# Expert weights in two mixtures: up matrices in 2 MB transfers into seven double buffers, down matrices in 1 MB transfers into seven single ones

## The chip, the cores and the metric

The kernel runs on one core of one Trainium2 chip. The metric is the device time of one execution in microseconds (us), lower is better; the median of three runs is given. MB stands for 1024 KB wherever buffers and transfers are counted; GB/s in the profile is decimal, so that one MB at 421 GB/s takes 2.49 us.

## What is computed

Two transformer blocks on 256 tokens of width 1024, all in float32. The part around the change is the mixture of experts that ends each block:

```
# block 1: 32 experts, hidden width 256, top-2 inside the best of 4 groups
hid = silu(einsum('td,edf->tef', t, w1)) * einsum('td,edf->tef', t, w3)
out = einsum('tef,efd->td', hid * gate, w2)
# block 2: 16 experts, hidden width 1024, top-2 inside the best of 4 groups
for e in range(16):
    h = silu(t @ w_gate[e]) * (t @ w_up[e])
    y = y + gate_dense[:, e:e + 1] * (h @ w_down[e])
```

Ahead of each mixture stands a token mixer: gated delta rule and spatial gating in block 1, stick-breaking and dilated attention in block 2. Ahead of block 1 and in the mixers, dense weights are loaded through the same buffers.

## The kernel before

**Work of a mixture.** Every expert is used, on the tokens routed to it. A **slice** is 256 hidden columns of one expert: 2 MB of up weights (both up matrices, in two halves of 1 MB by input rows) and 1 MB of down weights. Mixture 1 has 32 slices (96 MB), mixture 2 has 64 (192 MB). `mixture_steps` groups experts in units by how many tokens they hold: a **single** is one expert, a **pair** two, a **quad** four, and the experts of a unit work side by side on TensorE in 128, 64 or 32 columns. So a step costs TensorE about the same whatever its width, while it needs 3, 6 or 12 MB of weights. Mixture 1 has 11 steps, one for each unit: pair, pair, pair, quad, pair, quad, quad, pair, quad, quad, pair. Mixture 2 has 32 steps, four for each of its units: pair, pair, single, pair, quad, single, pair, pair. Steps are counted from 0. The first units hold "fixed" experts, known at build time; the others hold experts ranked by their load, and their numbers are read by SyncE with a `value_load` after VectorE has raised `order_ready`.

**Order on TensorE** (`mixture`, `up`, `down` in the tensor block): for step t it runs the first half of up(t+1), turns the hidden rows of t (L1143), at a new unit combines the outputs of the unit before and gathers the tokens of a later one, runs the second half of up(t+1), then down(t). The last combine is followed by a check of whether some expert has more than 64 tokens (`overflow`); here none has.

**Buffers** (`slot_table`). A ring of 11 slots of 1 MB, and nine other places of 1 MB that are free in a mixture: `x_ctx`, `heads`, `masks`, `head_w`, `tokens`, `squares`, `normed`, `routing`, `places` (the profile shows them as xc, o_heads, first_w, head_w, arena, hc, hc, arena, arena). That is 20 MB. `JOINS` says what such a place waits for when it is used first: `tokens` the residual of the mixer, `squares` and `normed` the norm ahead of the routing, `routing` and `places` the end of the routing itself. Every slot is freed when TensorE has run its last matmul on it: a counter `slots_used` counts slots in the order of use, and `FREE_AT` is the count that a load waits for.

**Loads** (`load_mixture`, `load_step`, L506). SyncE issues all weight loads in one fixed order, one by one, and waits in `slot_free` ahead of each that its slot is free; what stands behind a load that waits, waits too. The order is up(0), then for each t up(t+1) and down(t). Rows of a load are 8 KB long on each of 128 partitions. TensorE waits for the four (pair) or eight (quad) up slots of a step in two lots: first halves of all experts, then second halves. Dense weights of block 2 (16 loads) follow mixture 1 in the same queue, and the first loads of mixture 2 follow these.

```
for k in range(4):                                  # up(), each half of a step
    for j in range(wide):
        ins = mm(out[half, :], x[:, 4 * part + k, half], w[j][:, k, :], ...)
```

## Time and profile before

| | |
|---|---|
| median of three runs | 1599.21 us (1595.12 to 1599.33) |
| the profiled execution, its own time | 1599.86 us |
| its span in the trace | 1598.2 us |
| granted TensorE clock, mean | 0.98 |
| TensorE matmuls busy | 1480.7 us (93%) |
| VectorE, ScalarE, GpSimd busy | 511.2, 331.3, 152.2 us |
| bytes moved | 402.96 MB, of them 381.92 on SyncE's queue |

Busy time is the time in which an engine has an instruction under way. The views give microseconds from the start of the span. A row of the timeline has the start, how long the merged stretch lasts, the engine (PE is TensorE, DVE VectorE, ACT ScalarE, SPq SyncE's sequencer issuing transfers), the source line, operation, output and inputs, their shape, how many instructions it merges, and in brackets the idle time before it and what ended it. All matmuls written with the helper `mm` have line L679. A stretch of windows lists busy time and count of each engine, then the granted TensorE clock, the busy share of the 16 DMA engines and GB/s. The clock has two levels here, 1.0 (2.4 GHz) and 0.5 (1.2 GHz).

### The profile page before, as it was taken

What the parts mean: (1) busy time and instruction counts of PE and PEld (TensorE: products, weight loads), DVE (VectorE), ACT (ScalarE), POOL (GpSimd) and SP (SyncE); (2) the same over time, 40 slices, a digit from 0 to 9 for tenths busy, and PEclk for the clock granted to TensorE, in tenths of its full rate; (3) what the DMA queues carried; (4) which work ended last, traced back from release to release, by engine and by line L of the source; (5) the groups of instructions that cost most, each with busy time, mean ns of one, the idle gap of its engine ahead of it and who ended that gap; (6) DMA issues with size and microseconds to landing.
All of it is one profiled execution on the core that took longest, in us unless ns stands there. A gap on an engine that the chain in (4) does not pass through costs nothing.

```text
span 1598.2 us, 21336 instructions
## 1 busy us (share of the span) xinstructions
PE 1480.7 (93%) x8241; PEld 968.3 (61%) x8241; DVE 511.2 (32%) x1081; ACT 331.3 (21%) x725; POOL 152.2 (10%) x170
## 2 busy tenths in 40 slices
PE   6899999999999999989998789999999998579996
PEld 2577777777588888865554359967443543134433
DVE  2567777667631311153222110053401111001002
ACT  2343343443331100021110011152100000000001
POOL 1334433344200000000000000000000000000000
PEclk9999999999999999999999999999999999899999
DMA  9711111111754435429999996305699999999992
GB/s 381 315 54 39 52 39 39 39 52 39 294 223 156 158 132 185 160 93 372 421 420 422 421 415 239 132 1 190 269 421 421 421 421 422 421 421 421 422 420 122
DMA packets 58573, 402.96 MB, mean 252 GB/s; under 512 B 6801, under 2 KB 6929, under 8 KB 12288
## 3 DMA queue, kind: packets, MB, share of 16 engines
q1 hardware_dynamic: 52704, 381.92, 59.3%
q0 software_dynamic: 5792, 19.95, 4.1%
q8 instruction: 55, 0.90, 0.2%
q14 instruction: 22, 0.18, 0.0%
HBM read 400.75 MB, written 1.10 MB: 251 GB/s over the span
## 4 chain that ended last, share of the span: by engine, by line
PE 73%; SPq 9%; DMA 6%; DVE 5%; issue 2%; ACT 2%; POOL 1%; DVEq 0%; ACTq 0%; POOLq 0%
PE bank L679 72%; SPq L506 9%; DMA ring<-in_moe 4%; DMA first_w<-in_moe 2%; ACT arena L1435 1%; DVE arena L1874 1%; POOL arena L621 1%; PE bank L1143 1%; DMA xc<-in_xc 1%; DMA decay_rows<-arena 0%; ACT hc L1435 0%; DVE arena L1863 0%; DVE arena L1865 0%; DVE arena L1868 0%; DVE arena L1869 0%
## 5 line engine op out<-in xcount | busy, mean ns | idle before, releaser
L679 PE MATMUL bank<-arena 128*128 128x128 f32 (+6 forms) x3088 | 488.5, 326 | 34.9 <-DVE arena L1865 15.6
L679 PEld LDWEIGHTS bank<-arena 128*128 128x128 f32 (+3 forms) x3088 | 383.1, 184 | 163.1 <-issue 73.8
L1435 ACT ACTIVATE arena<-bank 128x256 f32<-128x256 f32 (+2 forms) x374 | 161.9, 448 | 1073.1 <-PE bank L679 797.9
L679 PE MATMUL bank<-ring,arena 128*64 128x512 f32 (+2 forms) x1288 | 330.6, 630 | 38.3 <-DMA ring<-in_moe 22.1
L679 PEld LDWEIGHTS bank<-ring,arena 128*64 128x64 f32 (+2 forms) x1288 | 99.1, 136 | 207.2 <-issue 206.5
L679 PE MATMUL bank<-hc,head_w 128*128 128x512 f32 (+1 forms) x384 | 161.6, 523 | 0.5 <-DVE hc L1798 0.5
L2218 DVE TENSOR_TENSOR arena<-arena,bank 128x256 f32<-128x256 f32 x43 | 18.1, 421 | 340.3 <-ACT arena L1435 340.3
L679 PE MATMUL bank<-arena,ring 128*128 128x256 f32 x416 | 93.2, 380 | 1.5 <-DVE arena L1993 1.2
L679 PE MATMUL bank<-hc,ring 128*128 128x256 f32 x416 | 91.2, 379 | 0.0
L679 PEld LDWEIGHTS bank<-arena,ring 128*128 128x128 f32 x416 | 78.7, 190 | 13.9 <-DVE arena L1993 1.6
L679 PEld LDWEIGHTS bank<-hc,ring 128*128 128x128 f32 x416 | 78.4, 190 | 11.1 <-issue 0.8
L679 PE MATMUL bank<-hc,arena 128*64 128x512 f32 (+2 forms) x216 | 79.5, 638 | 0.9 <-DVE arena L2214 0.9
L1435 ACT ACTIVATE arena<-arena 128x512 f32<-128x512 f32 (+4 forms) x140 | 66.5, 507 | 41.9 <-DVE arena L1815 25.3
L1895 DVE TENSOR_TENSOR arena<-bank,first_w 128x512 f32<-128x512 f32 x80 | 55.3, 692 | 55.4 <-PE bank L679 53.1
L679 PEld LDWEIGHTS bank<-hc,head_w 128*128 128x128 f32 x384 | 63.8, 192 | 14.5 <-issue 10.9
L679 PE MATMUL bank<-first_w,arena 128*64 128x512 f32 (+3 forms) x152 | 64.7, 558 | 6.6 <-DMA ring<-in_moe 5.2
L2214 DVE COPY arena<-bank 128x512 f32<-128x512 f32 x19 | 13.1, 692 | 169.5 <-PE bank L679 169.4
L679 PE MATMUL bank<-head_w,arena 128*64 128x512 f32 (+3 forms) x176 | 64.4, 505 | 1.1 <-DVE arena L2214 1.1
L1813 DVE SCALAR_TENSOR_TENSOR arena<-arena,vec 128x512 f32<-128x512 f32 (+1 forms) x72 | 65.0, 903 | 1.2
L626 POOL TENSOR_TENSOR arena<-arena,first_w 128x512 f32<-128x512 f32 x40 | 55.0, 1375 | 101.6 <-PE bank L679 60.4
L679 PE MATMUL bank<-o_heads,arena 128*64 128x512 f32 (+2 forms) x120 | 55.8, 609 | 3.2 <-DMA ring<-in_moe 2.3
L679 PE MATMUL bank<-xc,arena 128*64 128x512 f32 (+2 forms) x120 | 55.8, 609 | 0.0
(273 smaller groups left out, 1281.8 us busy)
## 6 DMA issues: line engine op xcount, KB each, us to landing
ring<-in_moe SPq DMA_DIRECT2D x161, 1024.0 KB, 23.4
ring<-in_dense SPq DMA_DIRECT2D x59, 1024.0 KB, 10.4
arena<-in_moe SPq DMA_DIRECT2D x40, 1024.0 KB, 24.2
hc<-in_moe SPq DMA_DIRECT2D x27, 1024.0 KB, 24.6
head_w<-in_moe SPq DMA_DIRECT2D x15, 1024.0 KB, 19.8
xc<-in_moe SPq DMA_DIRECT2D x15, 1024.0 KB, 26.8
o_heads<-in_moe SPq DMA_DIRECT2D x15, 1024.0 KB, 23.7
first_w<-in_moe SPq DMA_DIRECT2D x15, 1024.0 KB, 20.9
```

What stands on the lines that cost most here:

```text
L506: sp.dma_start(into, rows_[part % len(rows_)][:, at:at + GROUP]).then_inc(sem_, 16)
L621: nc.gpsimd.tensor_tensor(beta_half[1], beta_half[1], et[1], ALU.mult).then_inc(s["back_half"], 1)
L626: nc.gpsimd.tensor_tensor(levels[k % 2], coupling, times(M(f"off{k}"), TT), ALU.mult).then_inc(s["level_masked"], 1)
L679: return nc.tensor.matmul(out, lhsT, rhs_, start=start, stop=stop, **kw)
L1143: ins = nc.tensor.transpose(bank[4 + step_no % 2][:, f * P:(f + 1) * P], hid[step_no % 2][:, f * P:(f + 1) * P], M("ident"))
L1435: return nc.scalar.activation(out, in_, func, **kw)
L1813: link(stt(c3, src, wgt, c3, ALU.mult, ALU.add))
L1874: stt(flat(conv[0]), flat(conv[0]), float(P) ** -0.5, flat(norms[0]), ALU.mult, ALU.mult).then_inc(s["normed"], 1)
L1895: tt_(group_of(picked, g), grown(g), times(M(f"pick{k + 1}"), 4), ALU.mult).then_inc(s["picked"], 1)
L2214: cp(x_cols[u % 2][:, 4:8, :].rearrange("p a b -> p (a b)"), bank[7][:, :]).then_inc(s["x_copied"], 1)
L2218: tt_(hid[step_no % 2], act_h[step_no % 2], bank[4 + step_no % 2][:, FS:2 * FS], ALU.mult).then_inc(s["hid_ready"], 1)
```

## The change

- Up weights of one slice are loaded in one transfer of 2 MB (rows of 16 KB on each partition) by `load_up`, into one of seven **double** homes: five neighbouring pairs of ring slots (0-1, 2-3, 4-5, 6-7, 8-9), and `tokens` and `squares`, each now 2 MB (`squares` takes all of `hc`, so `normed` is gone). Down weights are loaded as before, 1 MB each, by `load_down`, into seven **single** homes: ring slot 10, `head_w`, `x_ctx`, `heads`, `masks`, `routing`, `places`. 7 x 2 + 7 = 21 MB.
- A double home is free when the second half of its slice has been used. In `up_view` both halves wait for the whole 2 MB, so the first half of a quad waits for 8 MB, and no longer for 4.
- `mixture_loads` sets the order of the loads: as before, but with down(2) of the first expert ahead of up(3), and in mixture 2 also up(3) of the first expert, down(2) of the second and down(3) of the first.
- `y_rows`, `act_h`, `hid` and `hid_T` have one buffer each where they had two; ScalarE and VectorE wait for the one buffer (`hid_ready`, `h_turned`, `combined`).
- VectorE waits for the last `combined` of a mixture behind the overflow check, and no longer ahead of it.

```diff
-UP_SLOTS = {"quad": 8, "pair": 4, "single": 2}
-DOWN_SLOTS = {"quad": 4, "pair": 2, "single": 1}
+DOUBLE = {home: (home, home + 1) for home in range(0, RING - 1, 2)}
+DOUBLE.update({"tokens": ("tokens",), "squares": ("squares",)})
...
+def mixture_loads(m):
+
+    steps = STEPS[m]
+    count = [WIDTH[step[0]] for step in steps]
+    turns = [("up", 0, j) for j in range(count[0])]
+    for t in range(len(steps)):
+        if t + 1 < len(steps):
+            turns += [("up", t + 1, j) for j in range(count[t + 1])]
+        turns += [("down", t, j) for j in range(count[t])]
+    sooner = [("down", 2, 0)] if m == 0 else [("down", 2, 0), ("up", 3, 0), ("down", 2, 1), ("down", 3, 0)]
+    at = turns.index(("up", 3, 0))
+    return turns[:at] + sooner + [turn for turn in turns[at:] if turn not in sooner]
...
+        for what, t, j in mixture_loads(m):
+            if what == "up":
+                take(double, ("up", m, t, j), ("up", m, t, j, 1))
+            else:
+                take(single, ("down", m, t, j), ("down", m, t, j, 0))
...
+            def load_up(m, step_no, j, row):
+
+                sem_ = slot_free(("up", m, step_no, j))
+                sp.dma_start(double_at(HOME["up", m, step_no, j]), row[:, 0:2 * GROUP]).then_inc(sem_, 16)
...
+                def up_view(step_no, j, part):
+                    what = ("up", m, step_no, j)
+                    pe.wait_ge(landed[HOME[what]], LANDED_AT[what])
+                    return double_at(HOME[what])[:, part * GROUP:(part + 1) * GROUP].rearrange("p (k f) -> p k f", k=4)
...
-                        w = [slot_view("up", step_no, wide * part + j).rearrange("p (k f) -> p k f", k=4) for j in range(wide)]
+                        w = [up_view(step_no, j, part) for j in range(wide)]
...
                 def silu(step_no):
-                    act.wait_ge(slots_used, SLOT["up", m, step_no, UP_SLOTS[steps[step_no][0]] - 1] + 1)
-                    act_fn(act_h[step_no % 2], bank[4 + step_no % 2][:, 0:FS], ACT.Silu).then_inc(s["silu_made"], 1)
+                    act.wait_ge(slots_used, USED["up", m, step_no, WIDTH[steps[step_no][0]] - 1, 1])
+                    if step_no >= 1:
+                        act.wait_ge(s["hid_ready"], tb + step_no)
+                    act_fn(act_h, bank[4 + step_no % 2][:, 0:FS], ACT.Silu).then_inc(s["silu_made"], 1)
...
-                    if u >= 2:
-                        act.wait_ge(s["combined"], ub + u - 1)
-                    act_fn(y_rows[u % 2][:, 0:512], bank[6][:, :], ACT.Copy).then_inc(s["out_rows_copied"], 1)
+                    if u >= 1:
+                        act.wait_ge(s["combined"], ub + u)
+                    act_fn(y_rows[:, 0:512], bank[6][:, :], ACT.Copy).then_inc(s["out_rows_copied"], 1)
...
-                dve.wait_ge(s["combined"], ub + UNITS[m])
                 n_links = link.n
                 with dve.If(overflow(dve, m)):
+                    dve.wait_ge(s["combined"], ub + UNITS[m])
                     every_token(m)
                 assert link.n == n_links
+                dve.wait_ge(s["combined"], ub + UNITS[m])
```

The order of instructions on SyncE's queue at the two places where a stream of loads starts again. **First place:** the start of mixture 1, from the last load ahead of the routing. Before (the shape is partitions x floats, so 2048 is 1 MB; `arena` is `tokens` in the first row and `routing`, `places` further on, `hc` is `squares` and `normed`; TENSOR_LOAD reads an expert's number):

```order
L506 DMA arena<-in_moe 128x2048
L517 TENSOR_LOAD arena
L517 ISA x2
L517 TENSOR_LOAD arena
L517 ISA x2
L517 TENSOR_LOAD arena
L517 ISA x2
L517 TENSOR_LOAD arena
L517 ISA x2
L506 ISA
L506 DMA hc<-in_moe 128x2048
L506 ISA
```

With the change, behind the four reads (4096 is 2 MB; `hc` is `squares`, the ring pairs are 4-5, 6-7, 8-9, `arena` is `routing`):

```order
L555 DMA hc<-in_moe 128x4096
L555 ISA
L555 DMA ring<-in_moe 128x4096
L555 ISA
L555 DMA ring<-in_moe 128x4096
L555 ISA
L555 DMA ring<-in_moe 128x4096
L560 DMA arena<-in_moe 128x2048
```

Where eight loads of 1 MB carried the up weights of the first quad, four loads of 2 MB carry them now, and the 1 MB load into `routing` stands behind the fourth of them. That fourth one goes into ring pair 8-9, which held up(1) of the first expert; the next two (into pairs 0-1 and 2-3) are up(4).

**Second place:** the start of mixture 2. Before:

```order
L506 DMA hc<-in_moe 128x2048
L506 DMA head_w<-in_moe 128x2048
L506 DMA ring<-in_moe 128x2048 x7
L506 DMA xc<-in_moe 128x2048
L506 DMA o_heads<-in_moe 128x2048
L506 DMA first_w<-in_moe 128x2048
L506 DMA ring<-in_moe 128x2048 x4
L506 DMA arena<-in_moe 128x2048
L506 DMA hc<-in_moe 128x2048 x2
L506 DMA head_w<-in_moe 128x2048
L506 DMA ring<-in_moe 128x2048 x2
```

With the change:

```order
L555 DMA ring<-in_moe 128x4096 x4
L560 DMA first_w<-in_moe 128x2048
L560 DMA head_w<-in_moe 128x2048
L555 DMA ring<-in_moe 128x4096
L555 DMA arena<-in_moe 128x4096
L560 DMA ring<-in_moe 128x2048
L560 DMA xc<-in_moe 128x2048
L560 DMA o_heads<-in_moe 128x2048
L555 DMA hc<-in_moe 128x4096
L560 DMA arena<-in_moe 128x2048 x2
L555 DMA ring<-in_moe 128x4096
```

The second `hc` row of before is `normed` used for the second time, behind the first use of up(0); what stands ahead of it comes to 18 MB. With the change 19 MB stand ahead of the two `arena` rows (`routing`, `places`), and the ring pair behind them is the first that waits for up(0) to be used.

## Rows read from the trace of the kernel before

**Rows 1.** Page, part 2: GB/s in 40 slices of 40 us
```profile
GB/s 381 315 54 39 52 39 39 39 52 39 294 223 156 158 132 185 160 93 372 421 420 422 421 415 239 132 1 190 269 421 421 421 421 422 421 421 421 422 420 122
```
**Rows 2.** Windows: both mixtures' streams; columns as under the table above
```profile
745.00:945.00 200.00, 178.64 (x1146) 95.98 (x1143) 39.39 (x90) 21.95 (x45) 0.00 (x0) 0.96 1.01 421
1145.00:1545.00 400.00, 367.64 (x1744) 154.82 (x1742) 37.74 (x88) 29.66 (x70) 0.00 (x0) 0.97 1.01 421
```
**Rows 3.** Timeline of SyncE's issues, from mixture 1's first load to its restart
```profile
598.54 0.33 SPq L506 DMA_DIRECT2D head_w<-in_moe  x1
...
692.33 0.42 SPq L506 DMA_DIRECT2D arena<-in_moe  x1
722.34 0.94 SPq L506 DMA_DIRECT2D hc<-in_moe  x2
```
**Rows 4.** Windows of 1 us at the restart of mixture 2's stream
```profile
1132.00:1133.00 1.00, 1.00 (x8) 0.35 (x6) 0.89 (x5) 0.00 (x0) 0.00 (x0) 1.00 0.92 123
1133.00:1134.00 1.00, 1.00 (x6) 0.29 (x4) 0.90 (x6) 0.00 (x0) 0.00 (x0) 1.00 0.46 180
1134.00:1135.00 1.00, 1.00 (x6) 0.14 (x2) 0.71 (x3) 0.00 (x0) 0.00 (x0) 1.00 0.98 418
```
**Rows 5.** Timeline of TensorE: second halves of steps 1 and 2, mixture 1
```profile
736.50 3.65 PE L679 MATMUL bank<-ring,arena 128*64 128x512 f32 x16
...
754.34 4.08 PE L679 MATMUL bank<-ring,arena 128*64 128x512 f32 x17
```
**Rows 6.** Timeline of TensorE: first half of mixture 1's last step
```profile
905.16 3.65 PE L679 MATMUL bank<-ring,arena 128*64 128x512 f32 x16 [1.35 <-DMA ring<-in_moe]
```
**Rows 7.** Timeline of SyncE's issues in mixture 2
```profile
955.70 0.33 SPq L506 DMA_DIRECT2D hc<-in_moe  x1
...
1105.84 26.16 SPq L506 DMA_DIRECT2D hc<-in_moe  x2
...
1137.34 1.02 SPq L506 DMA_DIRECT2D arena<-in_moe  x2
...
1288.08 14.73 SPq L506 DMA_DIRECT2D ring<-in_moe  x5
```
**Rows 8.** Timeline of VectorE: the instruction that raises order_ready in mixture 2
```profile
1134.60 0.17 DVE L2055 CAST arena<-arena 128x14 uint32<-128x14 f32 x1
```
**Rows 9.** Timeline of TensorE in mixture 2: slot rows, then steps 13 and 14
```profile
1135.02 1.98 PE L679 MATMUL bank<-arena,ones 128*128 128x512 f32 x4
...
1295.23 4.08 PE L679 MATMUL bank<-ring,arena 128*64 128x512 f32 x17
...
1306.05 7.09 PE L679 MATMUL bank<-ring,arena 128*64 128x512 f32 x32
```
**Rows 10.** Timeline of TensorE: the last step of mixture 2
```profile
1559.69 3.65 PE L679 MATMUL bank<-ring,arena 128*64 128x512 f32 x16 [0.94 <-DMA ring<-in_moe]
...
1568.24 0.44 PE L1143 MATMUL bank<-first_w,arena 128*128 128x128 f32 x2
1569.57 0.61 PE L679 MATMUL bank<-o_heads,arena 128*64 128x512 f32 x1 [0.89 <-DMA first_w<-in_moe]
```
**Rows 11.** Timeline of TensorE and VectorE: last combine of each mixture, and what follows
```profile
936.52 3.72 PE L679 MATMUL bank<-arena 128*128 128x256 f32 x16 [0.82 <-DVE arena L2226]
...
941.76 3.23 DVE L2299 SCALAR_TENSOR_TENSOR xc<-bank,mod,xc 128x256 f32<-128x256 f32 x8 [5.29 <-issue]
...
1574.01 3.72 PE L679 MATMUL bank<-arena 128*128 128x256 f32 x16 [0.79 <-DVE arena L2226]
...
1578.64 2.74 DVE L2391 SCALAR_TENSOR_TENSOR xc<-xc,bank 128x256 f32<-128x256 f32 x8 [4.68 <-PE bank L679]
```
**Rows 12.** Windows: the load of xc, in rows of 16 KB, at the start
```profile
5.00:6.00 1.00, 0.00 (x0) 0.00 (x0) 0.00 (x0) 0.00 (x0) 0.00 (x0) 1.00 1.01 426
5.00:8.00 3.00, 0.00 (x0) 0.00 (x0) 0.00 (x0) 0.00 (x0) 0.00 (x0) 1.00 1.01 423
```
**Rows 13.** Window: TensorE at half clock in the down part of step 9
```profile
920.00:927.00 7.00, 5.61 (x32) 1.49 (x32) 0.00 (x0) 0.00 (x0) 0.00 (x0) 0.54 1.01 421
```

More of the change, by code:

```diff
@@ new lines, in slots_in_order_of_use, with parts, take, join @@
+def slots_in_order_of_use(m):
+    steps = STEPS[m]
+    def parts(what, t):
+        n = WIDTH[steps[t][0]]
+        return [(what, m, t, j, part) for part in range(2 if what == "up" else 1) for j in range(n)]
+    uses = parts("up", 0)
+    for t in range(len(steps)):
+        if t + 1 < len(steps):
+            uses += parts("up", t + 1)
+        uses += parts("down", t)
+    return uses
+def slot_table():
+    dense = [("dense", g, 0) for g in range(FIRST_GROUPS + SECOND_GROUPS)]
+    uses = dense[:FIRST_GROUPS] + slots_in_order_of_use(0) + dense[FIRST_GROUPS:] + slots_in_order_of_use(1)
+    used = {what: n + 1 for n, what in enumerate(uses)}
+    home_of, landed_at, free_at, joins = {}, {}, {}, {}
+    filled = {home: base for home, (_, base) in SHARED_SEMS.items()}
+    single = [(home, 0) for home in range(RING)]
+    double = []
+    def take(free, what, last_use):
+        home, freed = free.pop(0)
+        filled[home] = filled.get(home, 0) + 16
+        home_of[what], landed_at[what], free_at[what] = home, filled[home], freed
+        free.append((home, used[last_use]))
+    def join(home, what, sem, value):
+        assert home_of[what] == home, (home, what, home_of[what])
+        joins[what] = (sem, value)
+    def paired(free):
+        at = dict(free)
+        pairs = [(home, max(at.pop(h) for h in of)) for home, of in DOUBLE.items() if all(h in at for h in of)]
+        return sorted(pairs, key=lambda f: f[1]), sorted(at.items(), key=lambda f: f[1])
+    for g in range(FIRST_GROUPS):
+        for at, home in ((RING, "x_ctx"), (G0 // BLOCKS, "heads"), (G0 // BLOCKS + 1, "masks")):
+            if g == at:
+                single.insert(0, (home, 0))
+        take(single, ("dense", g), ("dense", g, 0))
+    join("x_ctx", ("dense", RING), "modulated", 1)
+    join("heads", ("dense", G0 // BLOCKS), "gdn_normed", 4)
+    join("masks", ("dense", G0 // BLOCKS + 1), "gdn_normed", 4)
+    for m in range(2):
+        double, single = paired(single)
+        double += [("tokens", 0), ("squares", 0)]
+        single += [("routing", 0), ("places", 0)]
+        if m == 0:
+            single.insert(0, ("head_w", 0))
+        for what, t, j in mixture_loads(m):
[3 more added lines that the diff above has]
+                take(single, ("down", m, t, j), ("down", m, t, j, 0))
+        first_use = {}
+        for what, t, j in mixture_loads(m):
+            first_use.setdefault(home_of[what, m, t, j], (what, m, t, j))
+        join("tokens", first_use["tokens"], *(("rest_taken", 5 * KT), ("out2_made", KT))[m])
+        join("squares", first_use["squares"], *(("rows_copied", 4), ("ln_var", 1))[m])
+        join("routing", first_use["routing"], *(("slots_spread", 1), ("order_ready", 2))[m])
+        join("places", first_use["places"], *(("slot_rows_made", 2), ("slot_rows_made", 4))[m])
+        if m == 0:
+            join("head_w", first_use["head_w"], "sgu_taken", KT)
+            single += [(h, freed) for home, freed in double for h in DOUBLE[home]]
+            single = sorted([f for f in single if f[0] not in ("tokens", "squares", "routing", "places")], key=lambda f: f[1])
+            for g in range(FIRST_GROUPS, FIRST_GROUPS + SECOND_GROUPS):
+                take(single, ("dense", g), ("dense", g, 0))
+    return used, landed_at, home_of, free_at, joins
@@ L164 @@
+USED, LANDED_AT, HOME, FREE_AT, JOINS = slot_table()
 SECOND_G = FIRST_GROUPS
@@ L518, in rows_of @@
                     return [row_of(m, w, ranked, i) for w in who]
[L520 to L527 removed]
+                for what, t_, j in mixture_loads(m):
+                    row = rows_of(t_)[j]
+                    if what == "up":
+                        load_up(m, t_, j, row)
+                    else:
+                        load_down(m, t_, j, row)
             def load_all_tokens(m):
@@ L1158, in down @@
                         wide = WIDTH[kind]
-                        w = [slot_view("down", step_no, j).rearrange("p (f d) -> p f d", f=2) for j in range(wide)]
+                        w = [down_view(step_no, j) for j in range(wide)]
                         for f in range(2):
```

164 lines of the change are left out of this document (59 added, 105 removed).

## The prediction

> **What bounds the kernel now.** I read the page's GB/s line first: 421 GB/s without a gap through most of both mixtures, far less elsewhere [rows 1]. Then windows over the two stretches: the DMA engines' share is 1.01, and 421 GB/s is the mean of 200 and of 400 us, while TensorE is idle for 21 and 32 us in them [rows 2]. So each mixture ends when its weights have arrived, and its end can be written as a sum: the moment at which the stream of loads runs again after the routing, plus the MB that are left, at 2.49 us each. Three things can move it: when the stream starts again and with how much in place, whether it ever runs dry, and its rate. TensorE's own work lies inside, except behind the last loads.
>
> A load is not moving as soon as it is issued. Mixture 2's stream starts again with the second of the two `hc` loads, issued at about 1131.6; the three microseconds to 1135 carry 123, 180 and 418 GB/s [rows 4, 7], as much as full rate from 1133.2 on. I count 1.6 us from issue to full rate.
>
> **Mixture 1, the stream.** Before, 16 loads of 1 MB are issued from 598.5 to 692.3, and the next at 722.3 [rows 3], so the stream runs from 723.9 with 80 MB left: 80 x 2.49 = 199.2, to 923.1. Nothing runs dry [rows 2].
>
> With the change 17 MB are in place by then (up 0, 1, 2, down 0, 1 and one of down 2), which is 1 MB or **2.5 us less** to do. But the queue then holds `squares` and ring pairs 4-5 and 6-7, whose slices have been used, and behind them pair 8-9, which is free only when TensorE has run the second half of step 1: the sixteen matmuls at 736.5 to 740.1 [rows 5]. Six MB last from 723.9 to 738.9; the seventh starts at 740.1 + 1.6 = 741.7. **Dry for 2.8 us.** Then 5 MB are free (pair 8-9, `routing`, pair 0-1) and last until 754.2. Next is pair 2-3, which waits for the second half of step 2: sixteen of the seventeen matmuls from 754.3 on, to 757.9 [rows 5]; start at 759.5. **Dry for 5.3 us.** Before, each half was freed by itself, and eight loads could be out where the new order waits on one. Check: at 759.5 the order has 28 MB behind it and 68 left, 169.3 us, end at 928.8, which is **5.7 us later** than 923.1 (2.8 + 5.3 - 2.5 = 5.6).
>
> **Mixture 1, TensorE behind it.** Up(10) is followed in the queue by 4 MB of down(9), 10.0 us. Before, its halves landed apart; now TensorE starts it when all is there and runs first half, turn, combine, second half: 3.6 + 0.4 + 3.7 + 3.6 = 11.3 us [rows 6, 11]. Down(9) starts **1.2 us later** than its data.
>
> **Mixture 2, the stream.** Before: 18 loads from 955.7 to 1105.8 [rows 7], running from 1133.2 with 174 MB left, 433.3 us, end at 1566.5. With the change 19 MB are in place; `routing` is next and waits for `order_ready`, raised at 1134.8 [rows 8], so the stream runs from 1136.4, and `places` joins at 1137.0, when the slot rows are made [rows 9]. The second load of the ring pairs behind them is free too, so this start costs 3.2 - 2.5 = 0.7 us. The buffers are full again at the single unit, where TensorE takes only 3 MB a step. Up(16) of the second expert has 84 MB ahead of it, which arrive by 1136.4 + 65 x 2.49 = 1298.3. Its pair, 6-7, is freed by the second half of step 13, from 1295.2 to 1298.8 [rows 9]; start at 1300.4. Before, too, SyncE stands still in this place (five issues in 14.7 us) [rows 7], but with enough loads out to bridge it. Dry for 2.1 us. Four MB later, 1310.4, pair 0-1 waits for the second half of step 14: 1306.05 is two halves, the first of them frees it at 1309.6 [rows 9]; start at 1311.2, dry for 0.8 us. Left are 104 MB, 259.0 us: end at 1570.2, **3.7 us later**.
>
> **Mixture 2, TensorE behind it.** The last loads are up(31), two of down(30), two of down(31). Before, the second half of up(31) began at 1559.7 and down(31) at 1569.6, 9.9 us for 4 MB, each part on its data [rows 10]. Now both halves wait for 1559.7, and from there come two halves, a turn, down(30), a turn and the copy of the turned rows (1568.2 to at least 1569.1): 3 x 3.6 + 0.4 + 0.9 = 12.1 us. **2.2 us.**
>
> **VectorE's wait.** The last combines end at 940.2 and 1577.7; VectorE goes on at 941.8 and 1578.6 [rows 11], because it reads the count of tokens only then. With the change that read is done before. I take **-2.0 us**; at most 2.4, at least 0.8, as ScalarE and TensorE still do such a read of their own.
>
> **The rate.** Rows of 16 KB occur once, in the load of `xc` at the start: 423 GB/s over 3 us, 426 over the best of them, against 421 with rows of 8 KB [rows 12, 2]. So the gain on up weights lies between nothing and 1.2%; I take 1%, between the two windows. It counts only behind the last dry stretch, since what comes sooner ahead of one only lengthens it: two thirds of 68 + 104 MB, 114 MB or 284 us, **-2.8 us** (ends: 0 and -3.4).
>
> The Trainium skill, "DMA: Bandwidth & Descriptors", section Bandwidth, has a fixed 2 us for each transfer and 341 GB/s at 1 MB against 425 at 16 MB. By that, half as many up transfers would be worth many microseconds more than I take. This trace disagrees for queued loads: 1 MB loads back to back already run at 421 GB/s [rows 2].
>
> **Costs nothing:** the single `act_h`, `hid`, `hid_T` and `y_rows`. ScalarE's silu of t+1 needs the second half of up(t+1), which TensorE runs after the turn of t, so `hid_ready` and `h_turned` have come; copying outputs of a unit comes after a whole down, and the combine of the unit before stands ahead of it. If TensorE's order were another, each would cost the copy, 0.4 to 0.7 us a step. SyncE's issues halve for up weights; it only waits [rows 7].
>
> **Sum:** 5.7 + 1.2 + 3.7 + 2.2 - 2.0 - 2.8 = **+8.0 us**, on the profiled execution's own 1599.9, so 1607.9. That execution is 0.7 above the median of the runs, so I say **1607 us**.
>
> **Rivals.**
> 1. *Part of the delay is repaid* (0.21). TensorE waits in few long pieces in place of many short ones. In the down part of step 9 the granted clock was 0.54 over 7 us, right behind such a wait, which cost 7 x 0.46 = 3.2 us [rows 13]; with down(9) now behind 11 us of work instead of behind an idle time this can vanish, and a rate gain at its upper end adds 0.6: +4.2, about 1603.5, within 0.3%. Against it: new waits of over 10 us in the quads (8 MB is 20 us) are worse for the clock.
> 2. *Faster* (0.11): rows of 16 KB run clearly faster once the queue is full. Without the rate the sum is +10.8, and each percent gives 2.8 us, so the change breaks even at 3.9%, 437 GB/s, and is faster by over 0.3% from 5.6%, 445 GB/s; with 6% it would be 1593. For it: only 3 us of such rows were seen, beside other loads. Against: those read 423 and 426 [rows 12]. The Trainium skill, same page, section Bandwidth, gives 435 GB/s as the ceiling of the sixteen ports; by it this case ends below break-even.
> 3. *The rows are cut up and the rate stays* (0.07): +10.8, 1610.
> 4. *Colder* (0.11): each mixture's last steps hold one more such piece at half clock, 3.2 us each: +14.4, about 1613.5.
>
> **Chances.** The forecast has 0.50, and with rivals 3 and 4 slower has 0.68; no change 0.21, faster 0.11. A measurement of this kernel can tell about 0.3%, 4.8 us, from no change. The forecast's own range is 1604 to 1611 (rate 0 to 1.2%, VectorE's ends, each dry stretch a microsecond either way); taking in rivals 1, 3 and 4 the range is 1599 to 1614.
>
> **What would show it.** Right: GB/s falls short of 421 around 739 and 755, and around 1299 and 1311; the stream of mixture 2 starts again 3 us later than before; the last combine of mixture 1 begins some 6 us later, that of mixture 2 some 4 us later within its mixture; VectorE goes on at once behind them. In the quads of mixture 2 TensorE waits once a step for over 10 us in place of twice for 6. Wrong: no dip at those places (pairs free sooner than I count), a rate over 430 GB/s in the steady part, or mixture 1 ending no later than before.

## The result, and the profile after

| | before | with the change |
|---|---|---|
| median of the runs | 1597.9 us (5 runs, 1595.1 to 1599.3) | 1605.0 us (5 runs, 1601.8 to 1608.4) |
| ratio | | 1.0046, 95% interval 1.0033 to 1.0059 |
| the profiled execution, own time and span | 1599.86, 1598.2 us | 1601.81, 1600.1 us |

The change costs 7.3 us by the ratio (0.46%), 7.1 by the medians. A second set of six runs of the same kernel, later in the study, gave 1.0045 (1.0031 to 1.0060). The profiled execution of the changed kernel is the fastest of its five, so the two profiles differ by only 1.9 us where the medians differ by 7. I compare by stages, therefore, and not by spans.

The page's GB/s in 40 slices, changed kernel (it answers to [rows 1]):

```profile
GB/s 386 311 51 39 52 39 43 36 52 39 305 232 148 145 131 158 54 251 320 426 424 427 415 412 203 132 5 245 301 426 426 421 379 426 424 426 426 425 424 87
```

Two things are to be seen: the level of most full slices is 424 to 427 where it was 420 to 422, and two slices fall out of it, 320 (slice 19, 720 to 760; 372 before) and 379 (slice 33, 1280 to 1320). Windows show why: the places at which the forecast had the queue run dry or start late, and between them the two streams of [rows 2]. Columns are as there, the last two the DMA share and GB/s:

```profile
736.00:738.00 2.00, 2.00 (x12) 0.69 (x10) 0.00 (x0) 0.31 (x1) 0.00 (x0) 1.00 0.19 74
738.00:740.00 2.00, 2.00 (x12) 0.60 (x10) 1.79 (x6) 0.07 (x1) 0.00 (x0) 1.00 0.64 147
750.00:752.00 2.00, 2.00 (x19) 1.88 (x20) 0.08 (x1) 0.60 (x1) 0.00 (x0) 1.00 0.67 287
752.00:754.00 2.00, 2.00 (x10) 0.58 (x10) 0.61 (x1) 0.00 (x0) 0.00 (x0) 1.00 0.00 0
754.00:756.00 2.00, 2.00 (x12) 0.72 (x10) 0.05 (x1) 0.38 (x1) 0.00 (x0) 1.00 0.00 0
756.00:758.00 2.00, 2.00 (x12) 0.70 (x10) 1.89 (x6) 0.00 (x0) 0.00 (x0) 1.00 0.87 213
745.00:945.00 200.00, 176.98 (x1140) 95.92 (x1139) 39.37 (x90) 22.25 (x46) 0.00 (x0) 0.95 0.98 411
1132.00:1134.00 2.00, 2.00 (x8) 0.68 (x4) 0.97 (x4) 0.38 (x1) 0.00 (x0) 1.00 0.47 94
1134.00:1136.00 2.00, 2.00 (x10) 0.63 (x10) 1.76 (x4) 0.00 (x0) 0.00 (x0) 1.00 0.94 389
1145.00:1545.00 400.00, 360.98 (x1728) 152.69 (x1726) 37.48 (x87) 29.61 (x70) 0.00 (x0) 0.95 1.00 420
1294.00:1296.00 2.00, 2.00 (x12) 0.72 (x10) 0.00 (x0) 0.00 (x0) 0.00 (x0) 1.00 0.35 147
1296.00:1298.00 2.00, 2.00 (x12) 0.69 (x10) 1.10 (x4) 0.38 (x1) 0.00 (x0) 1.00 0.50 106
1298.00:1300.00 2.00, 2.00 (x12) 0.61 (x10) 1.81 (x5) 0.00 (x0) 0.00 (x0) 1.00 0.76 303
1308.00:1310.00 2.00, 2.00 (x13) 0.58 (x9) 0.07 (x1) 0.00 (x0) 0.00 (x0) 1.00 0.84 246
```

Counted as time at 426 GB/s that is missing: 2.9 us around 738, 5.7 around 754, 3.4 around 1297, 0.8 around 1309. The stream of mixture 2 is at full rate from 1133.7 (1136 less 483 x 2 / 426), and the mixture itself (VectorE's first gather instruction) began 2.5 us sooner in this execution, so against it the restart is some 3 us later than before. SyncE's issues in mixture 1 show the load on which the queue stands (answering to [rows 3]):

```profile
721.19 16.92 SPq L555 DMA_DIRECT2D ring<-in_moe  x3
738.22 0.37 SPq L560 DMA_DIRECT2D arena<-in_moe  x1
739.93 16.03 SPq L555 DMA_DIRECT2D ring<-in_moe  x2
756.22 0.33 SPq L560 DMA_DIRECT2D arena<-in_moe  x1
```

The third and the fifth of these ring loads are the ones that wait for a second half of a step, and downs behind them (L560) are issued at once when they are out: those had been free for longer.

Behind the streams, TensorE at the last up of mixture 2, and VectorE's last copy of mixture 1 and first operation after it (answering to [rows 10, 11]):

```profile
1558.46 1.09 PE L731 MATMUL bank<-hc,arena 128*64 128x512 f32 x1 [2.92 <-DMA ring<-in_moe]
```

```profile
936.07 0.69 DVE L2287 COPY arena<-bank 128x512 f32<-128x512 f32 x1 [7.43 <-PE bank L731]
940.58 1.66 DVE L2361 SCALAR_TENSOR_TENSOR xc<-bank,mod,xc 128x256 f32<-128x256 f32 x4 [3.81 <-PE bank L731]
```

TensorE waits for the whole 2 MB of a slice; VectorE goes on 4.51 us after the start of its last copy, released by TensorE. TensorE's waits for DMA after 700 us, in total, times, longest:

```profile
PE bank L731 <- DMA ring<-in_moe: 54.4, 8, 15.9
PE bank L731 <- DMA arena<-in_moe: 5.8, 1, 5.8
PE bank L731 <- DMA head_w<-in_moe: 2.6, 1, 2.6
```

Before, the ring's were 32.3 us in 10 waits, the longest 6.3:

```profile
PE bank L679 <- DMA ring<-in_moe: 32.3, 10, 6.3
```

### The profile page after: what moved, and what is told of

Same layout as the page of the kernel before. It is cut to its first block, busy times and chain, and to the rows that moved or that the text cites. A ratio compares the mean times of both kernels' runs of the same rounds, so it can differ in the third digit from the quotient of the medians.

```text
span 1600.1 us, 21159 instructions
## 1 busy us (share of the span) xinstructions
PE 1478.0 (92%) x8241; PEld 963.7 (60%) x8241; DVE 511.1 (32%) x1081; ACT 331.0 (21%) x725; POOL 152.2 (10%) x170
## 4 chain that ended last, share of the span: by engine, by line
PE 79%; DMA 10%; DVE 5%; issue 2%; ACT 2%; POOL 1%; SPq 1%; DVEq 0%; ACTq 0%; POOLq 0%
PE bank L731 78%; DMA ring<-in_moe 8%; ACT arena L1492 1%; PE bank L1200 1%; DVE arena L1933 1%; DMA head_w<-in_moe 1%; POOL arena L673 1%; DMA arena<-in_moe 1%; DMA xc<-in_xc 1%; ACT hc L1492 0%; DVE arena L1922 0%; DVE arena L1924 0%; DMA decay_rows<-arena 0%; DVE arena L1927 0%; DVE arena L1928 0%
## 5 line engine op out<-in xcount | busy, mean ns | idle before, releaser
L731 PE MATMUL bank<-arena 128*128 128x128 f32 (+7 forms) x3184 | 548.9, 335 | 47.6 <-DMA ring<-in_moe 20.8
L731 PEld LDWEIGHTS bank<-arena 128*128 128x128 f32 (+3 forms) x3184 | 399.3, 183 | 202.9 <-issue 116.6
L731 PE MATMUL bank<-ring,arena 128*64 128x512 f32 (+2 forms) x1232 | 336.7, 627 | 38.3 <-DMA ring<-in_moe 30.6
L731 PE MATMUL bank<-hc,arena 128*64 128x512 f32 (+1 forms) x208 | 101.0, 631 | 2.9 <-DMA ring<-in_moe 2.9
L731 PE MATMUL bank<-arena,ring 128*128 128x256 f32 x352 | 78.4, 380 | 1.5 <-DVE arena L2052 1.2
L731 PEld LDWEIGHTS bank<-hc,head_w 128*128 128x128 f32 x384 | 64.6, 194 | 16.8 <-issue 13.2
L731 PEld LDWEIGHTS bank<-arena,ring 128*128 128x128 f32 x352 | 66.6, 190 | 11.9 <-DVE arena L2052 1.6
L731 PE MATMUL bank<-head_w,arena 128*64 128x512 f32 (+2 forms) x168 | 60.6, 499 | 0.0
L731 PE MATMUL bank<-first_w,arena 128*64 128x512 f32 (+2 forms) x144 | 58.9, 539 | 1.6 <-DVE arena L1928 1.5
L731 PE MATMUL bank<-o_heads,arena 128*64 128x512 f32 (+2 forms) x112 | 50.5, 593 | 0.6 <-DMA first_w<-in_moe 0.6
L731 PE MATMUL bank<-xc,arena 128*64 128x512 f32 (+2 forms) x112 | 50.5, 593 | 0.0
## 6 DMA issues: line engine op xcount, KB each, us to landing
ring<-in_dense SPq DMA_DIRECT2D x60, 1024.0 KB, 10.5
```

Of the source, the lines that this page charges most:

```text
L731: return nc.tensor.matmul(out, lhsT, rhs_, start=start, stop=stop, **kw)
```

## The experiments

All were timed in five rounds, between runs of the kernel before (on these chips 1597.6 to 1597.8). Because the streams set the end, I also give the length of the mixtures themselves in each profile: from VectorE's first gather instruction to its last copy of outputs.

| kernel | median us | ratio to before, 95% | us | mixture 1, us | mixture 2, us |
|---|---|---|---|---|---|
| before | 1597.9 | | | 225.1 | 450.8 |
| the change | 1605.0 | 1.0046 (1.0033, 1.0059) | +7.3 | 228.0 | 455.7 |
| the change again | 1604.9 | 1.0045 (1.0031, 1.0060) | +7.2 | 228.2 | 455.9 |
| 1 wait put back | 1608.2 | 1.0057 (1.0043, 1.0071) | +9.1 | 230.6 | 455.9 |
| 2 two loads | 1608.7 | 1.0060 (1.0046, 1.0074) | +9.6 | 229.2 | 458.8 |
| 3 two waits | 1605.2 | 1.0041 (1.0027, 1.0054) | +6.6 | 227.3 | 457.1 |
| 4 list reordered | 1599.8 | 1.0013 (1.0004, 1.0022) | +2.1 | 226.2 | 452.4 |
| 5 two releases | 1598.1 | 1.0004 (0.9995, 1.0013) | +0.6 | 224.9 | 456.2 |
| 6 before, wait moved | 1595.9 | 0.9989 (0.9980, 0.9998) | -1.8 | 225.1 | 450.7 |
| 7 before, single buffers | 1597.6 | 1.0001 (0.9992, 1.0010) | +0.2 | 222.6 | 450.9 |
| 8 21 homes of 1 MB | 1589.0 | 0.9946 (0.9932, 0.9959) | -8.6 | 219.2 | 448.5 |
| 9 as 8, 16 MB ahead | 1594.4 | 0.9977 (0.9968, 0.9986) | -3.7 | 222.5 | 448.2 |
| 10 as 8, by slices | 1586.1 | 0.9930 (0.9917, 0.9943) | -11.2 | 217.5 | 448.3 |
| 12 as 5, reordered | 1595.9 | 0.9984 (0.9975, 0.9993) | -2.6 | 223.1 | 453.2 |

The column "us" is (ratio - 1) x 1597.7. Each has an interval of 1.4 to 2.2 us either way, and a difference of two has 2 to 3. One profile's mixture 1 can lie 2.5 us off another's of the same loads (kernels before and 7), see the last section.

**The change again** (experiment 11), unaltered.

> The changed kernel itself, on the chip of the last runs, as the foot of the ladder. Expected 1605, between 1603.5 and 1606.5.

**1. VectorE's wait put back.** The change, with

```
+                dve.wait_ge(s["combined"], ub + UNITS[m])
                 n_links = link.n
                 with dve.If(overflow(dve, m)):
-                    dve.wait_ge(s["combined"], ub + UNITS[m])
                     every_token(m)
-                dve.wait_ge(s["combined"], ub + UNITS[m])
```

> The changed kernel (1605.0) with VectorE's wait for the last combine put back ahead of the overflow check. Theory (the moved wait gave back about 2 us at the two mixture ends, the loads cost the rest): 1607, between 1606 and 1608, and in the trace the first VectorE operation after each mixture about 5.3 us after its combine's copy instead of 3.8. Rival (the check's value load was hidden anyway): 1605, no change.

It measured +1.8 against the change by the ratios (+3.2 by the medians, just above the expected range), where 2 was expected. The difference of two ratios is uncertain by 2 us or more, so this run alone doesn't show it. The profile has VectorE's operation after mixture 1 behind an idle time that nothing in the trace releases, 5.98 us after its last copy began:

```profile
940.27 0.69 DVE L2287 COPY arena<-bank 128x512 f32<-128x512 f32 x1 [7.43 <-PE bank L731]
946.25 3.23 DVE L2360 SCALAR_TENSOR_TENSOR xc<-bank,mod,xc 128x256 f32<-128x256 f32 x8 [5.29 <-issue]
```

**6. The kernel before, with only that wait moved** (the reverse edit).

> The kernel before with VectorE's wait moved into and behind the overflow check, nothing else. Theory: 1595.8, between 1595 and 1597, the first VectorE operation after each mixture's last combine 4.5 us after VectorE's last copy in both mixtures instead of 6.0 and 5.3. Rival (what lies between the mixtures absorbs it): 1597.8.

It measured -1.8 (interval -0.3 to -3.2), and in its profile the distance after mixture 1 is 4.51 us in place of the 6.0 of before, that after mixture 2 4.50 in place of 5.4:

```profile
935.23 0.69 DVE L2226 COPY arena<-bank 128x512 f32<-128x512 f32 x1 [7.43 <-PE bank L679]
939.74 3.23 DVE L2300 SCALAR_TENSOR_TENSOR xc<-bank,mod,xc 128x256 f32<-128x256 f32 x8 [3.81 <-PE bank L679]
```

Both sides and the distances in the traces agree: the moved wait is a gain of about 2 us, which the rest of the change hides.

**7. The kernel before, with single buffers.** `act_h`, `hid`, `hid_T`, `y_rows` as in the change, with its waits, for instance

```
-                    if u >= 2:
-                        act.wait_ge(s["combined"], ub + u - 1)
-                    act_fn(y_rows[u % 2][:, 0:512], bank[6][:, :], ACT.Copy)...
+                    if u >= 1:
+                        act.wait_ge(s["combined"], ub + u)
+                    act_fn(y_rows[:, 0:512], bank[6][:, :], ACT.Copy)...
```

> The kernel before with one act_h, one hid, one hid_T and one y_rows and the changed kernel's waits for them; loads as before. Theory (no step waits for them): 1597.8, between 1597 and 1599. Rival (the added waits of ScalarE and VectorE hold each step up by 0.1 us or more over 43 steps): 1602 or more.

+0.2, within 1.6 of nothing. The buffers that the change gives up had no use in this order of the work.

**2. Two loads for each double home.**

```
-                sp.dma_start(double_at(HOME["up", m, step_no, j]), row[:, 0:2 * GROUP]).then_inc(sem_, 16)
+                into = double_at(HOME["up", m, step_no, j])
+                for half in (slice(0, GROUP), slice(GROUP, 2 * GROUP)):
+                    sp.dma_start(into[:, half], row[:, half]).then_inc(sem_, 16)
```

(and 32 counts for an up's landing in the table)

> The changed kernel with each 2 MB up slice loaded as two transfers of 1 MB (rows of 8 KB) into the same double home, same order, freed and waited for as one. Theory (the rows of 16 KB are a gain of 1.2 percent on the queued stretches, hidden behind the loss): the steady rate falls from 426 to 421 GB/s, mixture 1 ends 2 us and mixture 2 3 us later, 1610, between 1608 and 1612. Rival (the rate does not matter or comes from the larger transfer being issued early, not from its rows): 426 GB/s stays, 1605. Rival (large transfers are the harm): 1600 or less.

1608.7, +2.3 us against the change by the ratios, +3.7 by the medians; the mixtures are 1.2 and 3.1 us longer than in the change's profile. Rows and issues are all that differ, and the page's level is back at 421:

```profile
GB/s 385 306 54 39 52 39 42 36 52 39 312 226 156 134 129 157 72 239 334 422 421 421 418 409 184 131 25 242 287 420 421 422 391 421 422 421 421 421 421 83
```

So the large transfers are a gain of about 1.2% in rate, and they are not what costs the time. Whether it is the longer rows or the fewer transfers that give it, this run can't tell: it changes both.

**3. Two loads, two waits.** Each half has its own count of landings, and `up_view` waits for its own part alone:

```
-                    pe.wait_ge(landed[HOME[what]], LANDED_AT[what])
+                    if part == 0:
+                        pe.wait_ge(landed[HOME[what]], LANDED_AT[what])
+                    else:
+                        pe.wait_ge(landed[LANDED_AT[(*what, 1)][0]], LANDED_AT[(*what, 1)][1])
```

> As the run before, with a semaphore for each 1 MB half, so that TensorE's first half of a step waits for the first halves alone; homes still freed as one. The loads stay in the slice order, so of a step of four TensorE still needs three and a half slices before it starts. Theory (landing granularity is the small part, 1 to 3 us at the ends of the mixtures): 1608, between 1606 and 1610, the last up of mixture 2 no longer waiting 2.9 us. Rival (landing of 2 MB at once is the main loss): 1602 or less.

It measured 1605.2, 0.8 below the range expected, and 3.0 us (ratios) or 3.5 (medians) below experiment 2, shared by both mixtures (1.9 and 1.7). The rival's 1602 was not reached. That the last up of mixture 2 would no longer wait did not come: TensorE waits 4.05 us there (4.79 in experiment 2).

**5. Two loads, two waits, two releases.** The first half of a home is free when the first half of its slice is used:

```
                 sp.dma_start(into[:, 0:GROUP], row[:, 0:GROUP]).then_inc(sem_, 16)
+                if FREE_AT[(*what, 1)] > 0:
+                    sp.wait_ge(slots_used, FREE_AT[(*what, 1)])
...
+            free_at[(*what, 1)] = freed
+            freed = first_freed[0] if first_freed else freed
+            free.append((home, used[last_use], used[(*last_use[:4], 0)]))
```

> The kernel with two transfers and two waits (1605.2), and now each half of a double home is also released by its own use: the first half by the first half of the step, one TensorE piece of 3.4 us to over 10 us sooner. Same order of the slices. Theory (the late release of first halves is the largest part of the loss): 1600.5, between 1599 and 1602.5; the dry stretch at 751 to 757 falls from 6 us to 3, those at 1294 to 1300 and 1308 to nothing. Rival (the order of the list, slices before halves, is the loss and the release is not): 1605.

1598.1, 5.9 us below experiment 3 by the ratios and 7.1 by the medians, sooner than the whole range that was expected. But the expected picture came only in part. Around 738 only 0.7 us is missing now (270 GB/s in 740 to 742), and 1.0 us near 1305 in place of the stretches at 1297 and 1309. The stretch at 752 to 760, which was to halve, is 5.4 us at 421 GB/s, as in experiment 3:

```profile
752.00:754.00 2.00, 2.00 (x18) 1.76 (x18) 0.21 (x1) 0.60 (x1) 0.00 (x0) 1.00 0.84 352
754.00:756.00 2.00, 2.00 (x12) 0.69 (x10) 0.48 (x1) 0.00 (x0) 0.00 (x0) 1.00 0.03 12
756.00:758.00 2.00, 2.00 (x12) 0.60 (x10) 0.18 (x1) 0.38 (x1) 0.00 (x0) 1.00 0.00 0
758.00:760.00 2.00, 2.00 (x12) 0.72 (x10) 1.86 (x7) 0.00 (x0) 0.00 (x0) 1.00 0.72 180
```

The list still goes slice by slice. The load of a first half goes out at 746.52, that of the second half behind it only at 757.50, and everything else stands behind it until then. The queue is one MB further when it stops, and that MB is the gain in mixture 1 (2.3 us in its stream, see the table of parts below). The gain of 6 to 7 us isn't to be found in the profile as a whole: the profiled execution is the slowest of the eleven (1600.9), and against experiment 3's its mixtures are 2.4 and 0.9 us shorter and the time between them 2.0.

**4. The change, with its list of loads reordered.** Homes, transfers and waits as in the change; downs with a free home go out ahead of an up that waits. In mixture 1 from step 1 on (u4.1 is the up slice of step 4's second expert):

```
+FIRST_LOADS = ("u0.0 u0.1 u1.0 u1.1 d0.0 d0.1 u2.0 d1.0 d1.1 u2.1 d2.0 u3.0 u3.1 d2.1 d3.0 u3.2 u3.3 u4.0 d3.1 d3.2 "
+               "u4.1 d3.3 u5.0 d4.0 u5.1 d4.1 d5.0 u5.2 u5.3 u6.0 d5.1 u6.1 d5.2 u6.2 d5.3 d6.0 u6.3 d6.1 u7.0 u7.1 "
...
+    for down, ahead_of in ((("down", 14, 0), ("up", 15, 1)), (("down", 15, 0), ("up", 16, 1)), (("down", 15, 1), ("up", 16, 3))):
+        turns.remove(down)
+        turns.insert(turns.index(ahead_of), down)
```

> The changed kernel with the same homes, 2 MB transfers and waits, and only the order of the load list changed, so that downs with a free home go out ahead of an up whose double home isn't released: in mixture 1 through most of the list, in mixture 2 three downs (steps 14, 15, 15). Theory (what costs is that the list blocks on a double home while single ones are free, so that the transfers run dry): the dry 6 us at 751 to 757 shrink to 2, those at 1294 to 1300 and 1308 to 1 together, 1597.5, between 1595 and 1600. Rival (fewer bytes can be in place whatever the order, since a double home is released 10 us later): dry stretches move but keep their sum, 1604 to 1606. Rival (single buffers make the steps slow): 1605.

1599.8: 5.2 us below the change, at the later end of what was expected. The transfers no longer stop around 754, but they do around 776, behind another up that waits:

```profile
752.00:754.00 2.00, 2.00 (x20) 2.00 (x20) 0.00 (x0) 0.31 (x1) 0.00 (x0) 1.00 0.96 410
754.00:756.00 2.00, 2.00 (x17) 1.59 (x18) 0.52 (x1) 0.28 (x1) 0.00 (x0) 1.00 0.97 410
776.00:778.00 2.00, 2.00 (x18) 0.56 (x12) 0.45 (x2) 0.38 (x1) 0.00 (x0) 1.00 0.00 0
```

At 426 GB/s some 6 us are missing in mixture 1's stream (3.5 of them at 772 to 780) where the change misses 9, and 2 where it misses 5 in mixture 2's. So the rival is half right here: the dry stretches move, but their sum shrinks. Mixture 1 is only 1.8 us shorter than the change's, mixture 2 3.3.

A home that is released sooner (experiment 5), or other loads sent ahead while it isn't (this one): by the medians either takes away most of the loss, and neither ends it.

**12. Both cures**: experiment 5 with the list of experiment 4.

> The two-frees kernel (1598.1) with the reordered list of the run that changed the order alone. Theory (two separate faults: the list, and homes split into ones for ups and ones for downs): the 3 us dry stretch at 753 to 757 vanishes, mixture 2 stays as it was, since there a down waits for the routing buffer from 1129 to 1134 with later homes free: 1595, between 1593.5 and 1596.5, and what is left against the kernel of 1 MB homes (1586.1) is the split. Rival (once halves are released by themselves the list no longer matters): 1598.

1595.9, 3.2 (ratios) or 2.2 us (medians) below experiment 5, as expected. Nothing is missing around 754, and 2.6 us at 776 to 784:

```profile
776.00:778.00 2.00, 2.00 (x16) 0.63 (x10) 0.85 (x3) 0.38 (x1) 0.00 (x0) 1.00 0.74 221
```

It stands where the kernel before stands with its wait moved (experiment 6, 1595.9).

**8. 21 homes of 1 MB.** The memory of the change, with `tokens` as two homes of 1 MB and `hc` as `squares` and `normed` again. Each home is loaded, waited for and released by itself. In mixture 1 two loads go ahead:

```
+    def parts(what, t):
+        n = WIDTH[steps[t][0]]
+        return [(what, t, j, part) for part in range(2 if what == "up" else 1) for j in range(n)]
...
+    moves = [[(('down', 2, 0, 0), ('up', 3, 0, 0)), (('down', 2, 1, 0), ('up', 3, 0, 0))], []][m]
...
+                 "tokens": area(5120, GROUP), "tokens2": area(5120 + GROUP, GROUP), "squares": flat(HS), "normed": flat(H),
```

> The changed kernel's memory (single buffers, tokens region of 2 MB, moved wait) but all homes of 1 MB, each filled by its own transfer, waited for and released by itself, halves in the order in which TensorE uses them (all first halves of a step, then all second ones), and in mixture 1 the two downs of step 2 ahead of step 3's first up, so that 18 MB stand in place before the routing is known. Theory (capacity helps, coarseness was the loss): against the kernel before -5 in mixture 1 (18 MB in place against 16), -2 in mixture 2 (one home more), -2 for the wait: 1589, between 1587 and 1592, at 421 GB/s. Rival (the added capacity lies where it isn't wanted): 1596, the wait's gain alone.

1589.0, as expected. The queue never runs dry and the rate is 421 from the first restart to the end:

```profile
GB/s 385 315 54 40 53 40 40 40 46 46 275 220 182 145 147 179 154 159 332 420 421 421 421 412 251 130 1 217 280 420 421 421 421 421 422 420 422 420 422 114
```

**9. As 8, without the two loads that go ahead.**

> The kernel of 21 homes of 1 MB (1589.0) without the two downs of step 2 ahead of step 3's first up in mixture 1: 16 MB in place before the routing is known instead of 18. Theory (mixture 1 is bound by the bytes left then, 2 MB at 421 GB/s are 5 us): 1594, between 1592.5 and 1595. Rival (the routing comes late enough that the two are made good by the ring): 1589.

1594.4, 5 us more, as 2 MB at 2.49 us say; mixture 1's stream is 5.0 us longer in the profile. What stands in place before the routing is known is worth its full transfer time. It is also a comparison with experiment 6: 1594.4 against 1595.9. That is 1.5 us by the medians and 1.9 by the ratios, no more than such a difference is uncertain by; mixture 2, where the 21st home was to give 2.5, is 2.5 shorter in the profile. The eleven executions here fall in two groups, five at 1591.5 to 1592.3 and six at 1594.4 to 1596.2.

**10. As 8, halves slice by slice** (`for j in range(n) for part in range(...)`).

> The kernel of 21 homes of 1 MB (1589.0) with the up halves loaded slice by slice as in the changed kernel, instead of all first halves and then all second ones. Theory (while the transfers never run dry the order within a step only moves TensorE's waits about): 1589 to 1590, the DMA's rows at 421 GB/s throughout; TensorE's longest wait 14 us instead of 6. Rival (the order of the halves is itself worth what the two-frees kernel lacked): 1591 to 1593.

1586.1: faster than expected by 2.9 us, and the best kernel of the study, 11.2 us below the kernel before. The theory was right that TensorE's waits change and wrong that the time doesn't. TensorE waits less often and longer:

```profile
PE bank L711 <- DMA ring<-in_moe: 20.1, 5, 6.4
PE bank L711 <- DMA hc<-in_moe: 13.8, 1, 13.8
PE bank L711 <- DMA head_w<-in_moe: 12.8, 1, 12.8
```

and at the end of mixture 1, where it works behind the last loads, the granted clock (third from the end) is 1.00, where experiment 8 has 0.89. Experiment 10, then experiment 8:

```profile
915.00:930.00 15.00, 13.42 (x76) 7.22 (x77) 2.64 (x5) 2.75 (x4) 0.00 (x0) 1.00 1.02 421
```

```profile
915.00:930.00 15.00, 12.75 (x67) 5.61 (x67) 1.38 (x2) 1.47 (x3) 0.00 (x0) 0.89 1.02 421
```

15 x 0.11 = 1.65 us, and mixture 1 is 1.7 shorter. I take the one for the other; with one profile of each it is not shown that the order of halves brings it (see the last section). The other 1.2 us lie between the mixtures (179.4 for 180.7 us), where the change itself shows either value in its two profiles. I can't say that the order causes that part.

## Why the prediction was right

The forecast was 1607, that is +8.0 us on a kernel before of 1599.2, with a loss as the likeliest case; it is 1605.0, +7.1 on 1597.9. The chain of experiments goes from the kernel before to the change in four steps, and each step can be set beside terms of the sum. (The steps add up to the change by construction; it is the single rows that bear on the forecast. The first step also holds the single buffers and the 21st MB.)

| terms of the prediction | forecast | measured by | by ratios (by medians) |
|---|---|---|---|
| both streams later | 5.7 + 3.7 = +9.4 | 3 against 6 | +8.3 (+9.3) |
| TensorE behind whole slices | 1.2 + 2.2 = +3.4 | 2 against 3 | +3.0 (+3.5) |
| VectorE's wait | -2.0 | 6 against before | -1.8 (-1.8) |
| rate | -2.8 | the change against 2 | -2.3 (-3.7) |
| sum | +8.0 | | +7.2 |

The profiles allow a finer account. Each mixture is three parts: from VectorE's first gather instruction to the full rate of the queue; the stream of loads from there until its last MB has moved, counted in windows of 2 us; and what TensorE does behind it, up to VectorE's last copy. Each part is good to some 0.3 us.

| profile | mixture 1: to full rate, stream, behind it | mixture 2 |
|---|---|---|
| before | 13.2, 199.2, 12.7 | 10.8, 433.9, 6.1 |
| 7 before, single buffers | 13.2, 199.1, 10.3 | 10.8, 433.9, 6.2 |
| the change | 13.6, 203.9, 10.5 | 13.8, 431.8, 10.1 |
| the change again | 13.6, 203.6, 11.0 | 14.0, 431.8, 10.1 |
| 3 two waits | 13.3, 204.8, 9.1 | 14.0, 434.2, 8.9 |
| 5 two releases | 13.2, 202.5, 9.1 | 14.2, 432.3, 9.8 |
| 12 as 5, reordered | 14.8, 199.1, 9.3 | 13.9, 431.5, 7.7 |
| 10 as 8, by slices | 13.3, 194.2, 10.0 | 10.8, 431.5, 6.1 |

The streams with their restarts were forecast, the rate taken off, 4.6 and 2.0 us later; they are 5.1 and 0.9 later (4.8 and 1.1 in the second profile of the change). That is the mechanism of the forecast, and it is right. What TensorE does behind them was forecast 1.2 and 2.2 longer and is 2.2 shorter and 4.0 longer. Here two effects of the clock enter that the sum does not have: the piece at half clock that the kernel before has at mixture 1's end and the change has not (3.2 us, rival 1), and one that the change has at mixture 2's end (1.7 us, part of rival 4). With both counted in, the forecast would be -2.0 and +3.9. So the good match of the total rests in part on luck: a gain and a loss that were priced as rivals are both in these profiles, and half cancel. By mixture the forecast was worse than its sum, +5.8 and +4.2 for +2.9 and +4.9, and its sign that mixture 1's last combine would come some 6 us later failed.

- **Mixture 1's stream.** The two dry stretches were put at 2.8 and 5.3 us and are 2.9 and 5.7. That pairs released by second halves are the cause was argued then. Experiment 5, which releases by halves, takes the first stretch away but for 0.7 us, and leaves the second, where a second half is still waited for in list order. Experiment 12, which also sends other loads ahead, takes the second away too (2.6 us are then missing at 776). So both bear on it, the late release and the list that waits on it.
- **Mixture 2's stream.** The restart was forecast 3.2 us later and came some 3 later; the dry stretches at 1298 and 1310, forecast at 2.1 and 0.8, are 3.4 and 0.8. The first is a microsecond more than worked out, about my margin; in the second profile of the change the two are 2.9 and 1.3.
- **TensorE behind it.** Measured in the mixtures' lengths, experiment 3 against 2: 1.9 and 1.7 us for the forecast's 1.2 and 2.2. Together right. Both have a granted clock of 0.86 in the last 25 us of mixture 2, so the difference is not the clock's. (4 MB are 10.0 us, so the forecast's own rows give 1.3 for its 1.2.)
- **VectorE.** Right, from both sides.
- **Rate.** I took 1% and the steady level rose by 1.2% (426 for 421), as the windows over `xc` had it [rows 12]. The idea that only bytes behind the last dry stretch count was not tested apart, but the dry stretches agree: the two around 1297 and 1309 are 4.2 us together in both profiles of the change and 3.0 in experiment 2, so about what the faster loads ahead of them gained. Experiment 2's mixtures put it at 1.2 and 3.1 us, with most of it in mixture 2, where 104 of the 172 MB lie. (Of what the prediction takes from the Trainium skill, the fixed 2 us of a transfer are not in the section that it names.)
- **The single buffers** cost nothing: shown by experiment 7.
- **Rival 1, the piece at half clock.** It was there in the profile before (0.54 over 7 us [rows 13]) and is gone in both profiles of the change: 1.00 from 912 to 932. So profiles differ in mixture 1 by only 2.9 us. Whether the change repays it is open. Experiment 7, which has the loads of the kernel before, shows 1.00 there too and a mixture 1 that is 2.5 us shorter, all of it behind the stream, with the same median. That speaks for a piece of chance in single executions, which I had read as a fixture of the kernel. But its buffers differ, the third profile of those loads (experiment 6) has 0.83 again, and the kernel before was profiled once only. The waits of over 10 us that I held against this rival came (15.9 us the longest).
- **Rival 4** came by half. Mixture 1's end is no colder, but over the last 25 us of mixture 2, counted back from VectorE's last copy in each profile, both profiles of the change have 0.93 where the one before has 1.00, 1.7 us. Experiments 1, 2, 3, 5 and 12 have 0.86 to 0.93 there too; experiments 4 and 6 to 10 have 1.00. It is the piece right behind TensorE's wait of 2.92 us: its first matmul takes 1.09 us (the row of 1558.46 above), those at full clock 0.59. In one fixed window, the change:

```profile
1550.00:1575.00 25.00, 21.60 (x94) 6.83 (x90) 0.84 (x2) 1.53 (x4) 0.00 (x0) 0.93 0.63 265
```

and before:

```profile
1550.00:1575.00 25.00, 20.82 (x95) 7.63 (x92) 1.53 (x3) 2.88 (x6) 0.00 (x0) 1.00 0.70 290
```

- **Rivals 2 and 3** did not come: the rate is 426, not 437 or 421.
- **What I had not seen** is how much was to be had. Against experiment 10 the change loses 18 to 19 us with the same 21 MB. By the runs: 2 to 3 of it come from the list (5 against 12), 6 to 7 from late release, 3 from whole-slice waits, less 2 to 4 for the rate. The rest, 8.6 to 9.8 (12 against 10), is the split into homes for ups and homes for downs, together with what experiment 10's order gives. Of this rest the traces show this much: 18 MB stand in place before mixture 1's routing where the pairs hold 17, and in mixture 2 the split one stops at a down that waits for the routing buffer, while ups behind it would have had free homes. Experiment 5 there, SyncE's issues:

```profile
1103.88 0.43 SPq L570 DMA_DIRECT2D hc<-in_moe  x1
1131.11 2.55 SPq L575 DMA_DIRECT2D arena<-in_moe  x2
1133.71 0.42 SPq L565 DMA_DIRECT2D ring<-in_moe  x1
```

and experiment 10, where loads go into the ring's next free homes while the routing is awaited:

```profile
1095.73 0.33 SPq L544 DMA_DIRECT2D hc<-in_moe  x1
1120.20 5.47 SPq L544 DMA_DIRECT2D ring<-in_moe  x4
1125.96 1.31 SPq L544 DMA_DIRECT2D arena<-in_moe  x2
```

Against the start of the mixture (1118.8 and 1111.0) the first of these stands at 12.3 us, the other at 9.2. Experiment 12's parts in the table above stand for experiment 5's here, with nearly the same restart in mixture 2. Set beside experiment 10's, mixture 1 is 5.7 us longer (1.5 to full rate; 4.9 in the stream, of which 2.5 are the one MB less in place and the rest the stop at 776; 0.7 shorter behind it), and mixture 2 is 4.7 longer (3.1 to full rate, 1.6 behind the stream, where the clock is 0.93 for 1.00). Why the first load behind the routing goes out some 1.4 us later in mixture 1 with the reordered list (experiments 4 and 12) was not looked into, and how much of the rest is the order of halves was not tested with split homes.

## What to carry to other kernels

In a stage that ends when its bytes have arrived, price a change of the loads as a sum over the queue: when it restarts and with how many MB in place, each stretch in which it is dry, the rate, and what runs behind the last transfer. A transfer twice as large was worth 1.2% in rate here. It pays only if what it is loaded into is still released as early, or if the list lets other loads pass while it isn't. And give a queue that is served in order one pool of equal homes: split by size, it stands still at one class while the other has room. Here that was up to 9 us, the order of the halves included.

## What the runs showed of the hardware that I had not expected

- Queued 1 MB transfers with rows of 8 KB ran at 421 GB/s in every kernel that has them, 2 MB transfers with rows of 16 KB at 424 to 427, steady over hundreds of microseconds. The Trainium skill, "DMA: Bandwidth & Descriptors", section Bandwidth, puts 1 MB at 341 and 16 MB at 425 GB/s, measured on transfers issued from GpSimd. For SyncE's queued loads the measurement decides, and shows 421 at 1 MB and 1.2% more at 2 MB.
- A piece at half clock can be there or not in the same place with the same loads: 912 to 932 us has 0.83 in the profile of experiment 6 and 1.00 in that of experiment 7, whose mixture 1 is 2.5 us shorter. The two kernels differ in their buffers and in VectorE's wait, so chance is likely and not shown. Until a kernel is profiled more than once, a stage of one profile is good to such a step only:

```profile
912.00:932.00 20.00, 15.60 (x77) 6.84 (x77) 2.42 (x5) 1.25 (x3) 0.00 (x0) 0.83 1.01 422
```

```profile
912.00:932.00 20.00, 17.12 (x94) 8.69 (x94) 2.42 (x5) 1.26 (x3) 0.00 (x0) 1.00 1.02 422
```
